# Experts: a quarter of the value rows weighted by ScalarE and summed by GpSimd instead of TensorE

## The reference

```python
def blk(xb):
    qh = (xb @ wq).reshape(PEER_BLOCK, PEER_HEADS, 2, PEER_DKEY // 2)
    s = jnp.einsum('thcd,hckd->thck', qh, keys).astype(jnp.float32)
    sv, si = lax.top_k(s, PEER_TOPK)
...
    gw = jax.nn.softmax(sc, axis=-1)
    hpre = jnp.einsum('td,thkd->thk', xb, u_tab[eidx])
    act = (jax.nn.gelu(hpre.astype(jnp.float32), approximate=False) * gw).astype(xb.dtype)
    return jnp.einsum('thk,thkd->td', act, v_tab[eidx])
```

## Time and profile before

| | us |
|---|---|
| median of 3 runs | 4672.85 |
| lowest and highest | 4672.67, 4673.74 |
| span of the profiled execution | 4669.5 |
| experts, from the first gather issued to the last dot started | 1995.7 to 4661.1 |

### The profile page before, as it was taken

How to read it: one execution, slowest core, us unless ns; L and a number is a source line. 1 busy time by engine, 2 the same in 40 slices (tenths; PEclk the granted TensorE clock), 3 DMA queues, 4 the chain that set the end, 5 groups by cost and what they waited for, 6 DMA issues and landing times.

```text
span 4669.5 us, 55429 instructions
## 1 busy us (share of the span) xinstructions
PE 4162.9 (89%) x18639; PEld 2493.3 (53%) x18639; DVE 2464.1 (53%) x5405; ACT 1744.9 (37%) x4663; POOL 1531.0 (33%) x1390
## 2 busy tenths in 40 slices
PE   7999999998687988889898898898898988988987
PEld 6888888886555764444344444443444443443331
DVE  2111111113743754377667667666676666676665
ACT  2111111113622654244444444444444444444443
POOL 0000000001524531044444444444444444444543
PEclk9999999998788999899999999999999999999999
DMA  8899899794497765689999999999999999999998
GB/s 282 282 323 320 295 324 309 263 302 159 156 348 248 233 182 199 239 376 427 427 427 422 427 422 417 423 424 419 420 421 422 423 415 422 424 420 417 420 418 369
DMA packets 320725, 1642.22 MB, mean 352 GB/s; under 512 B 44945, under 2 KB 88177, under 8 KB 178546
## 3 DMA queue, kind: packets, MB, share of 16 engines
q0 software_dynamic: 162640, 1160.06, 59.7%
q1 hardware_dynamic: 122202, 257.29, 16.2%
q10 hardware_dynamic: 35648, 222.04, 14.3%
HBM read 1550.47 MB, written 318.03 MB: 400 GB/s over the span
## 4 chain that ended last, share of the span: by engine, by line
DMA 30%; PE 18%; ACT 5%; issue 4%; DVE 1%; POOL 0%; DVEq 0%; POOLq 0%; ACTq 0%; PEldq 0%
DMA ex_rows<-scratch_uv,ex_E 30%; PE ex_ps_y L2876 14%; PE ex_ps_q L2824 3%; ACT ex_diag L2575 2%; ACT L2563 1%; ACT L2558 1%; ACT ex_w L2567 1%; ACT ex_gel L2563 1%; PE ex_ps_t L2786 1%; POOL ex_rows L2506 0%; PE ex_ps_y L2870 0%; ACT ex_ex L2558 0%; DVE ex_dots L2720 0%; DVE ex_rows L2720 0%; PE ex_ps_t L2810 0%
## 5 line engine op out<-in xcount | busy, mean ns | idle before, releaser
L2876 PE MATMUL ex_ps_y<-ex_rows,ex_diag 128*128 128x512 f32 (+1 forms) x4224 | 2016.6, 612 | 285.1 <-ACT ex_diag L2575 260.3
L2720 DVE CUSTOM_DVE_ANT_0 ex_rows<-ex_rows,ex_n2u 128x1024 f32<-128x1024 f32 x1056 | 1294.8, 1226 | 869.2 <-DMA ex_rows<-scratch_uv,ex_E 849.0
L2506 POOL DMA_INDIRECT ex_rows<-scratch_uv,ex_E x1056 | 1208.8, 1145 | 1529.5 <-PE ex_ps_y L2876 1385.9
L2876 PEld LDWEIGHTS ex_ps_y<-ex_rows,ex_diag 128*128 128x128 f32 (+1 forms) x4224 | 741.4, 189 | 1407.8 <-ACT ex_diag L2575 720.7
L412 PE MATMUL pj_ps<-pj_w_hi,pj_nT 128*128 128x470 f32 x3072 | 913.0, 377 | 6.5 <-DVE pj_w_lo L248 5.3
L2563 ACT ACTIVATE ex_gel<-ex_dots 128x1 f32<-128x1 f32 x1056 | 214.2, 203 | 1387.7 <-DVE ex_dots L2720 1385.5
L412 PEld LDWEIGHTS pj_ps<-pj_w_hi,pj_nT 128*128 128x128 f32 x3072 | 579.7, 189 | 88.7 <-issue 10.9
L412 PE MATMUL pj_ps<-pj_w_lo,pj_nT 128*128 128x470 f32 x1536 | 577.7, 376 | 0.0
L276 DVE COPY pj_zo<-pj_ps 128x470 f32<-128x470 f32 x96 | 61.3, 646 | 695.6 <-PE pj_ps L412 458.2
L2575 ACT ACTIVATE ex_diag<-ex_ident,ex_w 128x128 f32<-128x128 f32 x1024 | 411.1, 401 | 33.4
L276 ACT COPY pj_zo<-pj_ps 128x470 f32<-128x470 f32 x96 | 51.8, 553 | 786.5 <-PE pj_ps L412 419.1
(11 more groups left out here) (379 smaller groups left out, 3617.1 us busy)
## 6 DMA issues: line engine op xcount, KB each, us to landing
pj_w<-in_w_in POOLq DMA_DIRECT2D x24, 1880.0 KB, 17.5
scratch_z<-pj_zo SPq DMA_DIRECT2D x192, 235.0 KB, 11.3
scratch_uv<-in_peer_u ACTq DMA_DIRECT2D x8, 4096.0 KB, 25.4
scratch_uv<-in_peer_v ACTq DMA_DIRECT2D x8, 4096.0 KB, 43.3
scratch_uv<-in_peer_u ACTq DMA_DIRECT2D x4, 8192.0 KB, 43.1
scratch_uv<-in_peer_v ACTq DMA_DIRECT2D x4, 8192.0 KB, 74.7
out_dk_s<-in_cache_dil_k ACTq DMA_DIRECT2D x8, 4088.0 KB, 43.8
out_dv_s<-in_cache_dil_v ACTq DMA_DIRECT2D x8, 4088.0 KB, 55.8
```

Source lines behind the costliest of these rows:

```text
L2506: pool.indirect_dma_start(out=rows[:, p % SLOTS, :], out_offset=None, in_=d["uv"], in_offset=bass.IndirectOffsetOnAxis(ap=E[:, turn % 4, k ...
L2720: nc.vector.tensor_tensor_reduce(out=row, in0=row, in1=n2u[:, tile % 2], scale=1.0, scalar=0.0, op0=ALU.mult, op1=ALU.add, accum_out=dots[ ...
L2876: last = nc.tensor.matmul(y[0:n, 512 * c:512 * c + 512], diag[:, p % DIAGS, 0:n], rows[:, p % SLOTS, D + 512 * c:D + 512 * c + 512], start ...
```

## The change

A constant `POOL_AT = (1, 5, 9, 13)` names four steps of a turn. In every turn of the 8 full tiles except a tile's first one, the rows of these steps are pooled: ACT does not scale the identity for them but scales the `v` half of the row itself, in place in its slot; PE leaves them out; POOL adds them to `yo`, the output buffer (the first pooled row of a tile is copied, after the tile before has been stored). POOL does this immediately before it issues the gather that takes the slot again, 8 rows on, and then waits for its own addition. Before the last row of a tile PE waits for POOL's sum and adds `yo` to the accumulator with the identity in two matmuls. Counts of `diag` and `v_done` now go over the rows that PE sums.

```diff
--- before.py
+++ after.py
@@ -2392,6 +2392,7 @@
     TURNS = NT * PH + PH // PACK
     SLOTS = 8
     DIAGS = 4
+    POOL_AT = (1, 5, 9, 13)
     LOW = -3e38
     OUT_AT = [(0, 14)] + [(turn, k) for turn in (1, 2, 3) for k in (0, 8, 10, 12, 14)]
 
@@ -2438,6 +2439,7 @@
         E_done, ex_in, ex_out, er_done, gate_done = (sem(n) for n in ("E", "ex_in", "ex_out", "er", "gate"))
         row_in = [sem(f"row_in{i}") for i in range(SLOTS)]
         dot_done, gel_done, w_done, diag_done, v_done = (sem(n) for n in ("dot", "gel", "w", "diag", "v"))
+        scaled_done, pool_done = sem("scaled"), sem("pool")
 
         block = ctx.enter_context(nc.Block())
 
@@ -2458,6 +2460,28 @@
 
         def packs(turn):
             return turn >= NT * PH
+
+        def by_pool(turn, k):
+
+            return turn < NT * PH and not opens(turn) and k in POOL_AT
+
+        pooled = [by_pool(p // K, p % K) for p in range(TURNS * K)]
+        summed = [p for p in range(TURNS * K) if not pooled[p]]
+
+        def sums(p):
+
+            return sum(1 for u in summed if u <= p)
+
+        def pool_sums(p):
+
+            return sum(pooled[:p + 1])
+
+        def wait_freed(eng, p):
+
+            if pooled[p]:
+                eng.wait_ge(pool_done, pool_sums(p))
+            else:
+                eng.wait_ge(v_done, sums(p))
 
         def width(tile):
             return P if tile < NT else NS
@@ -2497,12 +2521,28 @@
 
         @block.gpsimd
         def _(pool):
+            def weighted_row(p):
+
+                tile, value = tile_of(p // K), rows[:, p % SLOTS, D:2 * D]
+                pool.wait_ge(scaled_done, pool_sums(p))
+                if pool_sums(p) > 1:
+                    pool.wait_ge(pool_done, pool_sums(p) - 1)
+                if pool_sums(p) == pool_sums(first_of(tile) * K) + 1:
+                    pool.wait_ge(keys_t, 2)
+                    if tile:
+                        pool.wait_ge(y_stored, 16 * tile)
+                    nc.gpsimd.tensor_copy(yo[:], value).then_inc(pool_done, 1)
+                else:
+                    nc.gpsimd.tensor_tensor(yo[:], yo[:], value, ALU.add).then_inc(pool_done, 1)
+
             for turn in range(TURNS):
                 pool.wait_ge(E_done, turn + 1)
                 for k in range(K):
                     p = turn * K + k
                     if p >= SLOTS:
-                        pool.wait_ge(v_done, p - SLOTS + 1)
+                        if pooled[p - SLOTS]:
+                            weighted_row(p - SLOTS)
+                        wait_freed(pool, p - SLOTS)
                     pool.indirect_dma_start(out=rows[:, p % SLOTS, :], out_offset=None, in_=d["uv"],
                                             in_offset=bass.IndirectOffsetOnAxis(ap=E[:, turn % 4, k:k + 1], axis=0)).then_inc(row_in[p % SLOTS], 16)
 
@@ -2568,15 +2608,20 @@
 
             def diagonal(turn, k):
                 p, j = turn * K + k, turn % 2
+                n = sums(p) - 1
                 act.wait_ge(w_done, p + 1)
-                if p >= DIAGS:
-                    act.wait_ge(v_done, p - DIAGS + 1)
+                if pooled[p]:
+                    value = rows[:, p % SLOTS, D:2 * D]
+                    nc.scalar.mul(value, value, w[:, j, k:k + 1]).then_inc(scaled_done, 1)
+                    return
+                if n >= DIAGS:
+                    act.wait_ge(v_done, n - DIAGS + 1)
                 if turn < NT * PH:
-                    nc.scalar.mul(diag[:, p % DIAGS, :], ident[:], w[:, j, k:k + 1]).then_inc(diag_done, 1)
+                    nc.scalar.mul(diag[:, n % DIAGS, :], ident[:], w[:, j, k:k + 1]).then_inc(diag_done, 1)
                 else:
                     if p == NT * PH * K:
                         act.wait_ge(fold_done, PACK)
-                    nc.scalar.mul(diag[:, p % DIAGS, 0:NS], fold[:], w[:, j, k:k + 1]).then_inc(diag_done, 1)
+                    nc.scalar.mul(diag[:, n % DIAGS, 0:NS], fold[:], w[:, j, k:k + 1]).then_inc(diag_done, 1)
 
             def outputs(tile):
                 act.wait_ge(y_sum, tile + 1)
@@ -2870,15 +2915,22 @@
                         last = nc.tensor.matmul(y[0:n, 512 * c:512 * c + 512], ident[0:n, 0:n], h[0:n, 512 * c:512 * c + 512],
                                                 start=True, stop=False, skip_group_check=True)
                     last.then_inc(h_used, 1)
-                pe.wait_ge(diag_done, p + 1)
+                if pooled[p]:
+                    return
                 end = closes(turn) and k == K - 1
+                if end and tile < NT:
+                    pe.wait_ge(pool_done, pool_sums(p))
+                    for c in range(2):
+                        nc.tensor.matmul(y[0:n, 512 * c:512 * c + 512], ident[0:n, 0:n], yo[0:n, 512 * c:512 * c + 512],
+                                         start=False, stop=False, skip_group_check=True)
+                pe.wait_ge(diag_done, sums(p))
                 for c in range(2):
-                    last = nc.tensor.matmul(y[0:n, 512 * c:512 * c + 512], diag[:, p % DIAGS, 0:n],
+                    last = nc.tensor.matmul(y[0:n, 512 * c:512 * c + 512], diag[:, (sums(p) - 1) % DIAGS, 0:n],
                                             rows[:, p % SLOTS, D + 512 * c:D + 512 * c + 512],
                                             start=False, stop=end, skip_group_check=True)
                 last.then_inc(v_done, 1)
                 if end:
-                    pe.wait_ge(v_done, p + 1)
+                    pe.wait_ge(v_done, sums(p))
                     pe.sem_inc(y_sum, 1)
 
             for turn in range(3):
```

## The result

The changed kernel takes 4678.92 us in the median of 20 runs (4672.59 to 4695.18), the kernel before 4673.64 us in 20 runs (4668.76 to 4679.35). The ratio is 1.0015, 95% interval [1.0009, 1.0021]: no change within the 0.2% that the prediction named, with a small loss that the many runs resolve. The profiled execution took 4672.59 us, its span is 4670.9 us. It is the fastest of the 20, so the small loss of the median can't be looked for in its trace.

The account below looks back on a forecast made before the run. The gather was taken as the bound. PE's relief counted 0 us and the added ACT, POOL and PE work 0 us, hidden by waiting rows: 0 on the median of 4672.85 us, so 4673 us, range 4662 to 4790 us.

Parts of the forecast that it names:

- The gather bounds the stage: Experts stage: fetching 1056 rows between 2004 and 4661 us, 2.52 us each, sets the time; a 16-row turn takes about 40 us.
- The rival that PE was the bound: Experts stage: PE, busy 0.89, limits after all, so the change gains at most 37 us, 4636 us; chance 0.07.
- The relief: PE skips 4 matmul records, 1.98 us, for each of 224 pooled rows: 444 us of PE, hidden behind the gather, worth 0.
- The line of waiting rows hides late slots: DMA queue: four rows stand in line, so each slot could come back about 10 us later before a DMA engine idles.
- The price of an addition: POOL, each pooled row: 2.5 us for the 128x1024 addition, plus 0.6 us waiting for a VectorE dot under way.
- The sum for a group of four rows: POOL per four rows: four issues 5.9, addition 2.5, wait for a dot 0.6, behind it 0.8: 9.8 of 10.0 us.
- the 0.8 us behind an addition: POOL: after an addition the waiting dot goes first and the next gather issue waits for it, 0.8 us.
- The rival that POOL becomes the bound: Issue behind each addition: groups above 10.36 us lose time, 99 us at 10.8 us, 144 us at 11.0; chance 0.27.
- The rival of late slots that add up: Lock, slow clock and ACT's exponent step coincide and empty the line: 0.4 us a turn, 22 us, 4695 us; chance 0.08.
- PE's wait for POOL's sum: Ahead of a tile's last row: costs nothing unless POOL is more than a row late.
- TensorE's clock: PE gaps of about 2.9 us bring 1.2 GHz stretches; a row's matmuls take up to 1.7 us longer, covered by the line.

Follow-up runs that it names:

- PE's relief alone: Changed kernel with its pooled rows left out of the sum (no ACT scaling, no POOL addition, no yo added by PE), 8 slots: 4674.23 us, 1.0008 of the kernel before.
- ballast: Kernel before, PE still summing every row, plus POOL adding four unscaled rows a turn to yo, sum thrown away: 4675.65 us, 1.0004 (8 slots); 1.0213 (6 slots).
- the variant with the clock kept up: Changed kernel plus two 512-column matmuls on PE at each pooled step, into the unused accumulator half: 4674.81 us, 1.0013 (8 slots); 1.0185 (6 slots).

## Why the prediction was right

- **The gather bounds the stage.** Right. 421 GB/s over 1000 us, before and after; the kernel before loses nothing with 6 slots. The DMA share of 1.01, on which the prediction leaned, would not have been enough: it reads 1.00 at 404 GB/s as well. PE's relief alone gives 1.0008. The rival that PE was the bound is out. The relief was also smaller than taken: 444 us were to go, less some 16 for adding the buffer, and 275 went, since the matmuls that sum rows, more of them at the lower clock, now take 644 ns in the mean instead of 612.
- **The line of waiting rows hides late slots.** Right, and shown from both sides: the change costs 1.0244 with 6 slots and 1.0015 with 8, the additions alone 1.0213 and 1.0004. The median time to landing is 12.3 us, inside the 10 to 13 us named.
- **The price of an addition.** 2.5 us was taken and 0.6 for the wait for a dot under way. Measured are 2.45 us in the mean with this wait in it; the median is 2.36 and the longest 3.71. So the wait exists, but it was put about six times too high: it comes to 0.1 us in the mean, because most additions find no dot ahead of them or go before it. The dot pays instead: 1.25 us per addition, inside the 1.1 to 2.5 us held.
- **The sum for a group of four rows.** 9.8 us was taken, of 10.0. With the pieces of the trace, 4 x (1.30 + 0.30) + 2.45 + 0.3 is 9.15 us, where 1.30 holds the longer issue behind an addition already. So the forecast that POOL would be "0.8 or more busy" failed: it is 0.72. The terms that were too large are the wait for a dot and the 0.8 us behind an addition: that issue takes 1.64 us, 0.34 above the mean of 1.30.
- **The rival that POOL becomes the bound.** It did not come with four rows and did with seven. Its formula undercounts: 194 us forecast, 235 measured for seven; 88 and 144 for six. It credits each tile with 10 us that POOL catches up in the opening turn. By the starts of the dots (turns 8 to 63) the opening turns get longer instead, 45.6 us with seven rows and 45.3 with six against 43.3 in the kernel before, and each other turn loses 3.8 us with seven rows (43.75 against 39.97), where 4.9 was taken. Also, the upper end of the range, 4790 us, belongs by this formula to 10.88 us a group, not 10.86.
- **The rival of late slots that add up.** It gave 22 us; the change costs 5. With 6 slots slots do come late, and it costs 111 us.
- **PE's wait for POOL's sum.** It was put at nothing unless POOL is more than a row late. Between 2400 and 4600 us PE did wait ahead of the last row seven times, 12.8 us in total, 2.8 at the longest. No run took this wait away.
- **TensorE's clock.** 0.95 in the stage (below 0.97 was named), PE 0.79 busy (about 0.75 was named). No cost shows with 8 slots, since the kernels with and without matmuls at the pooled steps lie at 1.0013 and 1.0015. The Trainium skill's advice against idle gaps between bursts of matmuls ("TensorE: Matmul & The Clock Gate", section "Why this matters for your kernels") holds for the speed of the matmuls, 3.56 against 1.98 us for a row. For the time it counts only once the slots are late: about 0.6 points with 6 slots.
- **GpSimd for elementwise additions.** The Trainium skill advises against it because GpSimd is the slower engine ("GPSIMD Engine Reference", section 4.1). No run here put the additions on VectorE, so that comparison was not tested. The price found, 111 us with 6 slots, comes from another side: POOL also issues the gathers, and its additions hold the dots.

**What stays open** is the loss of 5 us itself. Pooled rows left out (1.0008), ballast (1.0004) and the variant with the clock kept up (1.0013) have intervals that overlap each other and the 1.0015, so no part can be named. The page gives the packets of the gather queue 59.8% of 16 engines' span instead of 59.7%, with the same 162640 packets:

```profile
q0 software_dynamic: 162640, 1160.06, 59.8%
```

That 0.1% is of the size of the loss. But the ballast shows the same 59.8% at 1.0004 and the variant with the clock kept up 59.7% at 1.0013, so it proves nothing.

## What to carry to other kernels

Before work is moved off a busy engine, ask how long the data have been waiting for it: here rows stood 10 us in a DMA line, and relief of the engine behind the line was worth nothing. Such a line also hides what a change costs; take buffers away from both versions, and a price shows (here 111 us with two slots fewer) that is paid as soon as the line gets shorter. Work given to the engine that issues the transfers stands ahead of the next transfer with its own length, and the additions here, which read SBUF, also held VectorE's dots. A DMA share near 1 alone is no proof of a bound: 404 GB/s showed 1.00 and 384 GB/s 0.98, where 422 showed 1.01.

## What the runs showed of the hardware

- A VectorE dot and a GpSimd addition exclude one another here, and the earlier start in the trace does not decide who goes first. In 30 of 77 cases a dot with a start up to 0.63 us earlier was held (3.63 us instead of 1.23 in the one shown, with the addition unhurt at 2.35 us), and always by an addition that followed directly on an issue; with seven rows a turn this holds for all 127 dots that were held so. In others the addition was held, with a dot only 0.10 us ahead (3.33 us). The page "SBUF — State Buffer" of the Trainium skill (section "SBUF: two separate sides") says that whichever starts first gets the shared ports. By the starts in the trace that is not so within 0.63 us; whether the recorded start of an addition is later than the moment at which it takes the ports, no run shows.
- GpSimd fills of 1.82 and 0.96 us left the dots at 1228 ns in the mean. That only a GpSimd operation which reads SBUF excludes a two-input VectorE one is stated in the same section of the Trainium skill's page "SBUF — State Buffer", and this run agrees.
- Issues of indirect DMAs are held by a dot too: 0.94 us where no dot is near, 1.64 us directly behind an addition, where the dot that waited goes first. In the case shown the issue ends 0.82 us after the dot.
- ACT's scaling of 128x1024 in place, with its factor from SBUF, takes 1149 ns; the nearest row of another form has 1060.
